# A two-layer block with a hybrid mixer: the gated linear attention moved between the delta rule's projections, its output gates into the scans

## The reference, cut to what matters

```python
def step(s, inp):                      # run_gdn: gated delta rule
    u0_i, kcd_i, kd_i, gl_i = inp[:4]
    u = u0_i - jnp.einsum('bhcd,bhde->bhce', kcd_i, s)
    s_new = s * gl_i[..., None, None] + jnp.einsum('bhcd,bhce->bhde', kd_i, u)
    ...
    o = jnp.einsum('bhcd,bhde->bhce', qd_i, s) + jnp.einsum('bhcs,bhse->bhce', attn_i, u)
```

```python
def step(s, inp):                      # run_gla: gated linear attention
    kd_i, v_i, gl_i = inp[:3]
    s_new = s * gl_i[..., :, None] + jnp.einsum('bhcd,bhce->bhde', kd_i, v_i)
    ...
    o = jnp.einsum('bhcd,bhde->bhce', inp[3], s)
```

```python
y_gdn = (head_rmsnorm(og, gdn_norm_w) * jax.nn.silu(p['gdn_z'])).reshape(bb, l, GDN_V)
y_gla = (head_rmsnorm(ol, gla_norm_w) * jax.nn.silu(p['gla_g'])).reshape(bb, l, GLA_V)
return jnp.concatenate([y_gdn, y_gla], axis=-1).astype(dtype) @ w_out
```

## Time and profile before

| | us |
|---|---|
| median of 3 runs | 2494.01 (2489.74 to 2494.64) |
| profiled execution, its own time | 2495.68 |
| its span | 2493.9 |
| PE busy | 2314.1 |
| DVE busy | 1266.8 |
| ACT busy | 656.7 |
| PE in the chain that ended last | 77% of the span |

### The profile page before, as it was taken

One profiled execution on the slowest core, in us unless ns is written; L12 is line 12 of the kernel. 1 busy time (PEld: TensorE's weight loads), 2 busy tenths in 40 slices (PEclk: granted clock), 3 DMA queues, 4 the chain that ended last, 5 costly groups with the idle time before them and its releaser, 6 DMA issues.

```text
span 2493.9 us, 33513 instructions
## 1 busy us (share of the span) xinstructions
PE 2314.1 (93%) x14190; PEld 1922.1 (77%) x14190; DVE 1266.8 (51%) x2214; ACT 656.7 (26%) x855; POOL 57.1 (2%) x78
## 2 busy tenths in 40 slices
PE   6999979999989999899999999897799989989997
PEld 5858768799978578687998678884479977646996
DVE  3341246688633313344887335577455553644444
ACT  1113320043301133201343214122144421002442
POOL 0000000000000000000000000000010000000000
PEclk9999989999999999799999999988699999999999
DMA  6333225678643332356875321000165532203551
GB/s 214 143 118 118 102 93 211 230 248 280 204 123 135 118 118 102 134 211 223 277 267 172 105 71 69 2 2 34 34 197 186 185 134 78 101 1 110 186 186 68
DMA packets 206682, 348.62 MB, mean 140 GB/s; under 512 B 19587, under 2 KB 110474, under 8 KB 206149
## 3 DMA queue, kind: packets, MB, share of 16 engines
q1 hardware_dynamic: 191664, 291.09, 34.0%
q0 software_dynamic: 14592, 55.31, 6.6%
q10 hardware_dynamic: 276, 0.08, 0.0%
HBM read 345.41 MB, written 1.05 MB: 139 GB/s over the span
## 4 chain that ended last, share of the span: by engine, by line
PE 77%; DVE 16%; ACT 4%; issue 2%; DMA 1%; SPq 0%; DVEq 0%; ACTq 0%
PE psum L375 54%; PE psum L716 20%; DVE ring_low L1042 3%; DVE A L1506 3%; DVE G L1169 2%; DVE wide_room L1169 1%; ACT high_weights L1035 1%; ACT A L819 1%; DVE tmp L1169 1%; PE psum L434 1%; PE psum L420 1%; DMA ring<-in_w_in_dram 1%; PE psum L694 0%; DVE A L1169 0%; DVE xn L1469 0%
## 5 line engine op out<-in xcount | busy, mean ns | idle before, releaser
L375 PE MATMUL psum<-hT,ring 128*128 128x256 f32 (+2 forms) x3488 | 688.8, 359 | 9.4 <-DVE x L1169 5.1
L375 PEld LDWEIGHTS psum<-hT,ring 128*128 128x128 f32 (+1 forms) x3488 | 601.8, 195 | 86.0 <-DVE x L1169 6.9
L1042 DVE TENSOR_TENSOR ring_low<-ring,high_weights 128x2048 fp32r<-128x2048 f32 x124 | 284.2, 2292 | 171.5 <-ACT high_weights L1035 169.5
L716 PE MATMUL psum<-high_rows,high_weights 128*128 128x256 f32 x1280 | 365.0, 285 | 5.2 <-DVE ring_low L1042 5.2
L716 PE MATMUL psum<-high_rows,ring_low 128*128 128x256 f32 x1280 | 362.9, 284 | 0.0
L716 PEld LDWEIGHTS psum<-high_rows,high_weights 128*128 128x128 f32 x1280 | 243.1, 190 | 7.4 <-issue 6.7
L716 PEld LDWEIGHTS psum<-high_rows,ring_low 128*128 128x128 f32 x1280 | 245.5, 192 | 0.0
L1035 ACT ACTIVATE high_weights<-ring 128x2048 fp32r<-128x2048 f32 x124 | 237.8, 1918 | 3.9
L1506 DVE SCALAR_TENSOR_TENSOR A<-A,silu_c 128x256 f32<-128x256 f32 x392 | 190.1, 485 | 14.0
L716 PE MATMUL psum<-yT_low,high_weights 128*128 128x256 f32 x640 | 181.4, 283 | 0.0
L716 PE MATMUL psum<-x2T_low,high_weights 128*128 128x256 f32 x640 | 180.7, 282 | 0.0
(11 more groups left out here) (420 smaller groups left out, 2539.4 us busy)
## 6 DMA issues: line engine op xcount, KB each, us to landing
ring<-in_w_in_dram SPq DMA_DIRECT2D x36, 2048.0 KB, 7.7
ring<-in_ffn_w_dram SPq DMA_DIRECT2D x66, 1024.0 KB, 5.1
A<-in_mod_w_dram POOLq DMA_DIRECT2D x48, 1024.0 KB, 7.6
ring<-in_ffn_w_up_dram SPq DMA_DIRECT2D x44, 1024.0 KB, 5.2
ring<-in_ffn_w_down_dram SPq DMA_DIRECT2D x22, 1024.0 KB, 6.2
ring<-in_w_lift_dram SPq DMA_DIRECT2D x16, 1024.0 KB, 8.6
ring<-in_ab_w_in_dram SPq DMA_DIRECT2D x7, 2048.0 KB, 8.2
ring<-in_hy_w_in_dram SPq DMA_DIRECT2D x6, 2048.0 KB, 8.1
```

The costliest lines, as they stand in the source:

```text
L375: return pe.eng.matmul(out, lhsT, rhs, start=(k == 0), stop=(k == n - 1))
L716: ins = pe.eng.matmul(out, lhs[a], rhs[b], start=first and n == 0, stop=last and n == 2)
L1042: v.eng.tensor_tensor(low, whole, high.bitcast(F32), ALU.subtract).then_inc(*v.mark(f"w_lo/{l}.{i}"))
```

## The change

Nothing is computed otherwise in substance; three things are.

- **Order.** The panels come as `lv`, `small2`, `lqk`, `gk`, `gv`, `gq`, `lg`, `gz`. The whole gated linear attention of both sequences is cut into pieces and put between the halves of the delta rule's projections, on all three engines. Rooms in SBUF are assigned anew.
- **Fillers.** The 16 products of `lg` go into the scan of `s` = 0 and those of `gz` into that of `s` = 1: one before the update products of a step, two behind them, the rest behind the scan. They use fixed banks.
- **Smaller ones.** The keys' norm is taken by token (sums by ACT's accumulate on transposed keys, `keys_squared`; `keys_scaled` on DVE; turned back by `keys_back`), which drops the column sums and the wide root iteration on DVE. `llr` is one product of 48 rows in place of two of 16. The sums of `dec` for both sequences, and the gates, leave the stretches in front of the second inverse and scan. Two small DVE pieces come into the second inverse: the roots and `mixed(1, t)`, the head norm and gating of the linear attention.

```diff
-    plan = ["lv", "gk", "gv", "gq", "small2", "lqk", "lg", "gz", "ab_out.0", "ab_out.1"]
+    plan = ["lv", "small2", "lqk", "gk", "gv", "gq", "lg", "gz", "ab_out.0", "ab_out.1"]
...
+        def filler(name, first_bank):
+            w, used = panel(name)
+            left = [(t, k) for t in range(MT) for k in range(KD)]
+            banks_ = {}
+            def some(n):
+                for t, k in left[:n]:
+                    label = f"{name}_ready/1.{t}"
+                    if k == 0:
+                        banks_[t] = fixed(label, first_bank + t)
+                    ins = mm(banks_[t], hT[:, k, t * P:(t + 1) * P], w[:, k, :], k, KD)
+                    if k == KD - 1:
+                        ins.then_inc(*pe.mark(label, [used] if t else []))
+                del left[:n]
+            return some
...
+        w, used = panel("lqk")
+        transposed("lq", w, [], 1, 2, 0)
+        gla_gates(0)
+        transposed("lk", w, [], 0, 2, 256)
+        gla_gates(1)
+        transposed("lk", w, [used], 1, 2, 256)
+        w, used = panel("gk")
+        transposed("gk", w, [], 0)
+        gla_keys_turned(0)
+        transposed("gk", w, [used], 1)
+        gla_updates(0)
+        gla_keys_turned(1)
+        keys_turned(0)
+        w, used = panel("gv")
+        transposed("gv", w, [], 0)
+        gla_updates(1)
+        gla_logits(0)
+        keys_back(0)
+        keys_turned(1)
+        transposed("gv", w, [used], 1)
+        gla_outputs(0)
+        gla_logits(1)
+        keys_back(1)
+        for s in SL:
+            decays_summed(s)
+        w, used = panel("gq")
+        transposed("gq", w, [used], 1)
+        gla_outputs(1)
+        for s in SL:
+            values_turned(s)
...
-            if s:
-                for s_ in SL:
-                    gla_gates(s_)
+            some = filler(("lg", "gz")[s], (4, 6)[s])
             for i in range(NCHUNK):
...
+                some(1)
                 for d in range(2):
...
+                some(2)
+            some(16)
```

DVE's order in the first stage, and its pieces in the second inverse:

```diff
+        gate_numbers()
+        gla_gates(0)
+        gla_gates(1)
+        gla_cumulated(0)
+        gla_cumulated(1)
+        gla_products(0)
+        gates_made()
+        conv(0)
+        gla_products(1)
+        conv(1)
+        conv(2)
+        gla_states(0)
+        conv(3)
+        keys_scaled(0)
+        conv(4)
+        gla_states(1)
+        gla_masked(0)
+        conv(5)
+        keys_scaled(1)
+        conv(6)
+        gla_copied(0)
+        gla_masked(1)
+        for s in SL:
+            decays_copied(s)
...
+                    if s and (i, t) == (0, 1):
+                        root(rqg[:, 1, :], rqg[:, 0, :], rqg[:, 2, :], BD ** -0.5)
+                        heads_root(1)
+                    if s and i == 4:
+                        mixed(1, t)
```

More of the change, by code:

```diff
@@ L1786, in tensor_program @@
[L1786 to L1792, removed]
-            for t in range(MT):
[L1794 to L1801, removed]
@@ L1951, in tensor_program @@
                         ins.then_inc(*pe.mark(f"ou_ready/{key}"))
-        w, used = panel("lg")
-        tokens("lg", w, [used], 1)
-        for s in SL:
+                some(2)
+            some(16)
+        for n in (1, 0):
             for t in range(MT):
[L1958 to L1997, removed]
-                                                G[hh, d, c * SEQ + k * CHUNK:c * SEQ + (k + 1) * CHUNK],
-                                                G[hh, 17 + i, (2 * d + c) * P:(2 * d + c + 1) * P],
-                                                start=False, stop=True, skip_group_check=True)
-                ins.then_inc(*pe.mark(f"gla_o_ready/{t}.{e}"))
@@ new lines, in silu, with gla_softplus @@
+        def silu(n):
+            name, s = seqs[n // 2]
+            if n == 8:
+                a.wait_ge(*reached("gla_state/1.3.1"))
+                a.wait_ge(*reached("gla_att_ready/1.1"))
+            silu_of(a, n, seqs, rooms)
+        def gla_softplus(s):
+            a.wait_ge(*reached(f"gla_abs/{s}"))
+            z = rooms_of(s, 14)
+            copy(z, z, func=ACT.Exp)
+            e.activation(z, z, ACT.Ln, bias=one).then_inc(*a.mark(f"gla_soft/{s}"))
+            a.wait_ge(*a.own())
@@ new lines, in gla_updates_kept, with keys_squared @@
+        def gla_updates_kept(s):
+            if s:
+                a.wait_ge(*reached(f"gla_state/0.{NCHUNK - 1}.1"))
+            for c in range(NCHUNK):
+                label = f"gla_up_ready/{s}.{c}"
+                copy(G[:, 10 + c, :], take(label), f"gla_up/{s}.{c}", ["read " + label])
+        def keys_squared(s):
+            for t in range(MT):
+                b = take(f"gkt_ready/{s}.{t}")
+                for h in range(4):
+                    c = 8 * s + 4 * t + h
+                    e.activation(xn[:, 1, 512:512 + P], b[:, h * P:(h + 1) * P], ACT.Square,
+                                 accum_out=heads[:, 0, c:c + 1]).then_inc(*a.mark(f"gk_sq/{s}" if (t, h) == (1, 3) else None))
+                    a.wait_ge(*a.own())
@@ new lines, in heads_squared @@
+        def heads_squared(n):
+            for t in range(MT):
+                a.wait_ge(*reached(f"o_sum/{n}.{t}"))
+                for h in range(4):
+                    c = 8 * n + 4 * t + h
+                    e.activation(xn[:, 1, 512:512 + P], mix_room(n, t)[:, h * P:(h + 1) * P], ACT.Square,
+                                 accum_out=heads[:, 0, c:c + 1]).then_inc(*a.mark(f"head_sq/{n}.{t}" if h == 3 else None))
+                    a.wait_ge(*a.own())
+        for s in SL:
+            copy(llrT[:, s, :], take(f"llr_ready/{s}")[0:48, 0:SEQ], f"llrT/{s}", [f"read llr_ready/{s}"])
@@ L2445, in dve_program @@
+        e.memset(o_gdn[:, :, :], 0.0).then_inc(*v.mark())
+        v.wait_ge(*v.own())
+        for s in SL:
             if s:
```

568 lines of the change are left out of this document (315 added, 253 removed).

## The result

The changed kernel takes **2469.8 us** (median of 4, 2467.4 to 2471.1) against 2494.3 (median of 4); the ratio is 0.9895, interval 0.9872 to 0.9917. It is faster by 1.05%. The forecast was 2467, range 2444 to 2485. The profiled execution took 2467.4 us, with a span of 2465.6.

A forecast was written before the change was run, and what follows sets the result against it. PE bounds the kernel (77% of the chain), DVE mattering only where PE waits. Terms -79.7 + 39 + 7.8 + 6.2 + 0 = -26.7 from 2495.7 give 2469.0, less 1.7 to the median: 2467 us, range 2444 to 2485.

The forecast's parts named there:

- The tail: From the scan's end to the closing projection: 97.0 us before, 17.3 after, a gain of 79.7 us.
- First stage, PE's work: PE's own work in the first stage at full clock: 138.5 us against 124.9 before, +13.6.
- First stage, waits: PE waits on DVE, 2.4 us after the first `gk` pass and 5.8 at `gv` of the latents: +8.2 together.
- First stage, clock: Lower clock around the first stage's small products and outputs costs +17 us, bounds 3 and 24.
- The full-clock rival: Clock holds but in the outputs: first stage +25, second scan -3, 2450 us in all; chance 0.20.
- First scan: Scan of `s` = 0 with fillers: longer steps, six fillers and the queries' sums behind; +7.8 us.
- Second inverse: The roots and `mixed(1, t)` on DVE make PE wait near its start and twice at its end: +6.2 us.
- Second scan: Gates leave, fillers enter, a step takes 12.0 us at full clock: 0 change, bounds -3 and +5.
- Bank order: Rival: a first-stage wait like the 5.8 comes three more times, or fillers cost full length (+7): 2484 us; chance 0.20.
- No change: Rival: scans and inverse give back all that hiding the linear attention gains, needing +36 us against 14 counted; chance 0.02.
- The slower case: Rival: projection banks wait for ACT in each of ten halves; 4 us each gives 2507 us; chance 0.03.
- some 5 us: First stage: by the skill page's table-load cost, six added switches ahead of `gla_ks/0` would worsen the sum this much.

The follow-up runs named there:

- the two exchanges: Changed kernel with token tile 0's masks ahead of the states of `s` = 1, and turned-key products of `s` = 0 ahead of `s` = 1's cumulated decays: 2469.7 us.
- The experiment: Changed kernel without fillers in the first scan, all 16 products of `lg` behind the scan of `s` = 0: 2477.1 us, ratio 0.9922.
- The scan with the wait filled: Changed kernel with two fillers per step of the second scan moved ahead of its last `ou` product group, where PE waits: 2462.4 us, ratio 0.9862.
- three changes of order: Changed kernel with roots and `mixed(1, t)` behind the second inverse, second-scan fillers in the wait, and tile 0's masks ahead of `s` = 1's states: 2446.5 us.

## Why the prediction was right, step by step

- **The tail** (-79.7 forecast, -79.2 measured) was right in each piece: `gz` at +2.3, eight squares 3.4, root 2.4, six gatings 4.3, turn and spread 4.3. It is three times the net gain, and the only place with a gain.
- **First stage, PE's work** (+13.6): with the measured +34.4, less 10.5 of waits and 11.1 of clock, 12.8 remain. The difference is in the outputs, 4.8 us for a tile in place of 5.2.
- **First stage, waits** (2.4 and 5.8, +8.2): 2.53 and 7.08, and one that I had not named, of 0.93: together 10.5. Cause and place are shown by the two exchanges: each wait went with its own. The second was 1.3 larger, since I had DVE in the states of `s` = 1 without the 2 us that it waits there for ACT's copies.
- **First stage, clock** (+17): the total is mis-sized, and its parts more so. Measured against the same groups at full clock: `gab` and `lq` 5.1 (I had 1.7), turned keys and the next pass 1.8 and the start of `gv` 1.7 (I had 1 and 3.5 for updates and turns), `dec` and `gq` 2.5 (I had 7.8 with the first outputs), second outputs 0 (3). In all 11.1. The outputs, at 0.50 in the tail of before, ran at 1.00 between dense passes, 4.8 us for a tile. That a group was slow in one surrounding did not carry over. The full-clock rival was right on these and wrong on `gab`.
- **First inverse** (0, measured +1.4): I had named no term here. The wait ahead of it and the products before that come to nearly the same sum (10.1 us, before 9.9), but the same 736 records took 30.7 us in place of 29.4, at a granted clock of 0.91 in place of 0.95. Why it was lower is open.
- **First scan** (+7.8, measured +6.1): steps 6.1 to 6.6 for 6.65, and `kk` at full clock gave 2.1 for 1.3. The experiment shows that of ten products, 8.7 us, 4.3 were hidden.
- **Second inverse** (+6.2, measured +8.8): three waits at the forecast places, 1.70, 2.47 and 1.66. Mis-sized: the roots 2.4 (1.5) and the gating 5.1 (4.7), and 1.2 of half clock at the start that I had not counted.
- **Second scan** (0, measured +3.0): the step that failed is "a step at the full clock ... 12.0". It was 13.78. The fall of the clock behind DVE's bank wait, which I allowed for once or twice, came in every step, and just on the fillers (3.1 to 3.4 us for 1.74). The scan with the wait filled ran at 1.00 and confirms it.
- Errors of +4.6 and +1.7 on one side and -2.6, -3.0, -1.4 and -0.5 on the other nearly cancel. That the time was hit within 3 us is in part luck; the terms are right only within 5 each.
- **The rivals.** Bank order: one large wait came, not four; but its other half, fillers at their full length, nearly held in the second scan (8.1 of 8.7). No change: the inverses and scans gave back 19.3 us, not 36. The slower case needed ACT's reads to hold every half; ACT was late at none. The row for a table load, 1.28 us with the next function directly behind, held: in the changed kernel one starts at 1432.26 and its function at 1433.55. The Trainium skill (ScalarE: Activation LUTs, What ACT_TABLE_LOAD costs) has 1.38 us of draining besides; the trace of this kernel shows none. The prediction's "some 5 us" for six added switches is an estimate without a working; six times the 1.38 us of the Trainium skill's page would be 8.3.

## What to carry to other kernels

An independent product is cheap in an in-order program where the engine would wait: in the second scan ten fillers, six of them behind a step's products, cost 8.1 of their 8.7 us; with two of each step's three put ahead of the product that waits for a bank, twelve cost 0.4, the waits and the clock that no longer fell taken together. When a whole stage is moved under dense work, look afterwards for each single wait that it leaves and for what stands ahead of the releasing operation on its engine; here three changes of order were worth nearly as much again (23.3 us in the median) as the change itself (24.5). Ask of such a change whether the engine whose order it alters then waits itself: 2.8 us of idling on DVE came back as 4.6 on PE.

## What was unexpected of the hardware

The same 128 small records behind the same waits took 9.21 us at a granted clock of 0.83 and 12.18 at 0.61, in kernels that differ only in what came tens of us earlier. What sets the clock there no run shows. The same happened to the 128 records at the start of the second inverse: 5.16 to 6.70 us in thirteen kernels, with a wait of 4.76 or 4.77 ahead in each. Differences of up to 3 us in a stretch are therefore no evidence for an edit unless the clock beside them is the same.
